# Expert phases of a two-block kernel: how 32 gathered rows are brought in, turned and multiplied

## The chip, the cores and the metric

The kernel runs on one core of one Trainium2 chip. The metric is the device time of one execution in microseconds; the median of three runs is 3614.87 us (3610.04 to 3619.33). Times inside the program come from one profiled execution, whose own time is 3593.02 us, with a span of 3591.0 us from its first instruction to its last.

## The reference, cut to what matters

The program is two transformer blocks in float32. The first block has two layers; each ends in a mixture of experts. Tokens (768 in layer 0, 512 in layer 1; model width 1024) each go to 2 of 32 experts; an expert has three matrices, two of 1024x512 and one of 512x1024:

```
def expert_block(a):
    xb, e = a
    return (jax.nn.silu(xb @ w1[e]) * (xb @ w3[e])) @ w2[e]

yb = lax.map(expert_block, (buf.reshape(n_blocks, MOE_BLOCK, d), blk_e)).reshape(n_blocks * MOE_BLOCK, d)
return jnp.zeros((t, d), h.dtype).at[tok_s].add(w_s[:, None].astype(h.dtype) * yb[dest])
```

How tokens are grouped into blocks is free as long as each token meets its own two experts.

## The kernel before

Program order: projections and attention of layer 0, routing, experts; the same for layer 1; then the second block. Only the two expert phases (function `expert_phase`), the load of the down weights (`load_down`, L1327) and one line at the end of routing (L1493) are touched.

Work of an expert phase is cut into units: one unit is 32 token slots of one expert. An expert has as many units as it needs, at least one. For each expert the weights w1, w3 and w2 (2 MB each) are read from HBM into one of four slots. SyncE issues the loads (L1321 for w1 and w3, L1327 for w2), in order: the loads of expert i wait until expert i-4 has finished with its slot (semaphores `hidden` and `multiplied`). The first three experts' loads are already issued in the routing phase. w1 and w3 are laid out so that a partition takes 8 neighbouring rows, 16 KB in one piece; w2 so that a partition takes 4 rows that lie 128 rows apart, 4 KB each.

One unit runs over the engines like this:

- GpSimd gathers 32 rows of `f` from HBM with one indirect DMA (L1565), 4 KB to each of 32 partitions; two buffers `xg` lie side by side on partitions 0 to 31 and 32 to 63. It is three units ahead of the one that TensorE works on.
- VectorE copies the rows to `x` (L1654), which frees the buffer. TensorE turns them, eight 32x128 transposes into PSUM (`turn_x`, L1600). ScalarE copies one half to `xT` (L1636), VectorE the other (L1658).
- TensorE multiplies with w1 and w3 into `pH` (L1615): 64 matmuls in the trace, four 32-column strips of the array at a time, so that hidden columns 0 to 127 stand on partitions 0 to 31, the next 128 on 32 to 63, and so on.
- ScalarE takes the silu (L1644), VectorE multiplies (L1668) into `hh`. TensorE turns `hh` as one 128x128 transpose (L1622), VectorE copies it to `hT` (L1671).
- TensorE multiplies with w2 into `pY` (L1627, 32 matmuls), ScalarE copies `pY` to `y` (L1648), and GpSimd scatters it to HBM (L1570): 128 pieces of 1 KB from 128 partitions.

TensorE turns the rows of the next unit between `pH` and `pT` of this one. The order on each engine is the order of the code; the loops run to counts read from `unit_end`, which routing has computed.

Of the kernel before, what the change touches and what calls it, by code (L numbers as in the profile page):

```python
# [18 lines left out]
ALU = mybir.AluOpType  # L19
# [1304 lines left out]
def load_down(sp, g, l, i, e):  # L1324

    b = i % SLOTS
    sp.dma_start(slot_of(g, "w2", b)[:], g["moe_w2"][l, e].rearrange("(k p) n -> p k n", p=P)).then_inc(g["w2_in"][b], 16)  # L1327


def routing_phase(nc, g, l, nt, logits, share, gather_at, scatter_at, unit_end):  # L1330
# [4 lines left out]
    with Phase(nc) as ph:  # L1335
# [68 lines left out]
        def _(dve):  # L1404
# [88 lines left out]
            dve.tensor_copy(gather_at[:, 0:NU], table[:, 0])  # L1493
# [7 lines left out]
def expert_phase(nc, g, l, nt, gather_at, scatter_at, unit_end):  # L1501


    T = nt * P
# [3 lines left out]
    half = C // 2  # L1508
    YW = D // STRIPS
    w13_in, w2_in = g["w13_in"], g["w2_in"]  # L1510
    with Phase(nc) as ph:
        at_x = ph.sb("at_x", [P, 2], I32)
        at_y = ph.sb("at_y", [P, 2], I32)
        xg = ph.sb("xg", [2 * UNIT, D])
        x = ph.sb("x", [UNIT, D])
# [3 lines left out]
        hT = ph.sb("hT", [P, P])  # L1519
        y = ph.sb("y", [P, 2, YW])  # L1520
        pX = [ph.ps(f"pX{h}", [P, 512]) for h in range(2)]
        pH = ph.ps("pH", [P, 512])
        pT = ph.ps("pT", [P, 512])
        pY = ph.ps("pY", [P, 512])
        x_ready, x_turned, x_movedA, x_movedD, hidden, silu, gated, h_turned, h_moved, multiplied, y_moved, order = (
            ph.sem(n) for n in ("x_ready", "x_turned", "x_movedA", "x_movedD", "hidden", "silu", "gated", "h_turned", "h_moved",
                                "multiplied", "y_moved", "order"))
        mark = ph.sem("mark")
# [3 lines left out]
        ident = g["ident"]  # L1532
# [25 lines left out]
        def _(pool):  # L1558
            last_row, last_out = pool.to_reg(T - 1), pool.to_reg(2 * STRIPS * T - 1)
            step = Steps(pool, order)  # L1560
            y_rows = g["y"][0:2 * T, :].rearrange("t (s n) -> (t s) n", s=STRIPS)

            def gather(u, b):
                step(pool.tensor_copy(at_x[:, b:b + 1], gather_at[:, ds(u, 1)]))  # L1564
                pool.indirect_dma_start(out=xg[strip(b)], out_offset=None, in_=g["f"][0:T, :],  # L1565
                                        in_offset=bass.IndirectOffsetOnAxis(ap=at_x[0:UNIT, b:b + 1], axis=0),
                                        bounds_check=last_row, oob_is_err=False).then_inc(x_in[b], 16)
# [11 lines left out]
            pool.wait_ge(x_ready, 1)  # L1579
# [16 lines left out]
        def _(pe):  # L1596
            def turn_x():
                for k in range(C):
                    j = k % half
                    last = pe.transpose(pX[k // half][:, j * UNIT:(j + 1) * UNIT], x[:, k::C], ident[0:UNIT, 0:UNIT])  # L1600
                last.then_inc(x_turned, 1)

            pe.wait_ge(x_ready, 1)
            turn_x()
            start = 0
            for i in range(NE):
# [3 lines left out]
                with pe.Fori(start, end) as u:  # L1610
                    pe.wait_ge(x_movedA, u + 1)
                    pe.wait_ge(x_movedD, u + 1)
# [5 lines left out]
                    pe.wait_ge(x_ready, u + 2)  # L1618
                    pe.sem_inc(mark, 1)
                    turn_x()  # L1620
# [12 lines left out]
        def _(act):  # L1633
            def move_x(n):
                act.wait_ge(x_turned, n)
                act.activation(xT[:, 0:half].rearrange("p k n -> p (k n)"), pX[0][:, 0:half * UNIT], ACT.Copy).then_inc(x_movedA, 1)  # L1636

            move_x(1)
            n = pairs_of(act)
            with act.Fori(0, n) as p:  # L1640
                for b in range(2):
# [3 lines left out]
                    move_x(u + 2)  # L1645
# [1276 lines left out]
```

## Time and profile before

| what | us |
|---|---|
| median of the runs | 3614.87 |
| profiled execution, its own time | 3593.02 |
| its span | 3591.0 |
| TensorE busy with matmuls, of the span | 3081.0 (86%) |
| expert phase of layer 0, about | 640 to 1201 |
| expert phase of layer 1, about | 1690 to 2222 |

A busy TensorE is one whose matmul records cover the time; it says nothing on how much of the array works. In the expert phases it covers less of the time than elsewhere, and the DMA engines, mostly idle in the rest of the program, are busy without a break. In the rows below, "idle before" is how long an engine did nothing before an instruction, and the name behind the arrow is what ended that. GB/s is all that the core's 16 DMA engines moved; their share can be a little over 1 since packets overlap. PEclk (the column "clock") is the granted clock of TensorE, 1.00 being 2.4 GHz.

### The profile page before, as it was taken

To read this page: it belongs to the slowest core of one execution; us is meant where nothing else is said; L and a number is where in the kernel's file an instruction comes from. 1 tells how busy PE (TensorE), PEld (TensorE's weight loads), DVE (VectorE), ACT (ScalarE), POOL (GpSimd) and SP (SyncE) were. 2 spreads that over 40 slices of the span, in tenths; PEclk is the share of its full clock that TensorE was granted. 3 is DMA by queue.
4 is the path that set the end of the run, shared out by engine and by line. 5 is a ranking of instruction groups with operands and counts; after the bars stand their busy time and mean duration, and the time that the engine had idled before them with its cause. 6 is when DMAs were issued, how large, how long until landed. Compare 5 with 4: busy or idle time off the path is not lost. (4 is left out here: it accounts for less than half of the span.)

```text
span 3591.0 us, 53246 instructions
## 1 busy us (share of the span) xinstructions
PE 3081.0 (86%) x22053; PEld 1770.0 (49%) x22053; DVE 1072.3 (30%) x2287; ACT 793.6 (22%) x1605; POOL 496.4 (14%) x608
## 2 busy tenths in 40 slices
PE   7998897878779699885978665599999999999999
PEld 4556654555446445653655443344444554444444
DVE  3425855211111333655111111543220321211101
ACT  2225630111112322630111111321111231110100
POOL 0004610222223100530222221000000000000000
PEclk8999997989889899996999887699999999999999
DMA  7823004999998541005999996321221111322337
GB/s 294 316 103 110 1 36 182 392 395 395 388 392 320 214 117 63 31 19 234 387 388 394 402 393 267 121 71 67 82 70 71 69 49 70 106 71 71 117 105 257
DMA packets 213104, 684.90 MB, mean 191 GB/s; under 512 B 51439, under 2 KB 92843, under 8 KB 196551
## 3 DMA queue, kind: packets, MB, share of 16 engines
q1 hardware_dynamic: 201126, 655.66, 49.0%
q0 software_dynamic: 11808, 26.78, 2.2%
q8 instruction: 132, 2.16, 0.2%
q14 instruction: 38, 0.30, 0.0%
HBM read 653.89 MB, written 33.98 MB: 192 GB/s over the span
## 5 line engine op out<-in xcount | busy, mean ns | idle before, releaser
L1615 PE MATMUL pH<-w,xT 128*32 128x256 f32 x7552 | 482.3, 411 | 161.0 <-DMA w<-in_moe_w 160.0
L1615 PEld LDWEIGHTS pH<-w,xT 128*32 128x32 f32 x7552 | 302.8, 119 | 322.2 <-issue 224.9
L2675 PE MATMUL banks<-hT,wf 128*128 128x512 f32 (+2 forms) x768 | 303.2, 557 | 3.3 <-ACT hT L2732 2.8
L1668 DVE TENSOR_TENSOR hh<-hs,pH 128x128 f32<-128x128 f32 x118 | 34.0, 288 | 833.9 <-ACT hs L1644 833.9
L1627 PE MATMUL pY<-w,hT 128*32 128x256 f32 x3776 | 230.3, 384 | 60.6 <-DVE hT L1671 51.3
L923 POOL TENSOR_SCALAR E<-E,st 128x768 f32<-128x768 f32 (+3 forms) x80 | 168.2, 2102 | 659.7 <-DVE st L1173 659.1
L2675 PEld LDWEIGHTS banks<-hT,wf 128*128 128x128 f32 x768 | 140.8, 190 | 164.6 <-issue 154.9
L416 PE MATMUL pa<-aT,w 128*128 128x512 f32 x416 | 207.6, 604 | 1.3 <-DVE aT L680 1.3
L1627 PEld LDWEIGHTS pY<-w,hT 128*32 128x32 f32 x3776 | 131.8, 110 | 124.3 <-issue 70.4
L2421 PE MATMUL pa<-hT,ring 128*128 128x512 f32 x384 | 167.8, 592 | 0.0
L2326 PE MATMUL pa<-hT,ring 128*128 128x512 f32 x384 | 165.0, 592 | 1.3 <-PEq L91 1.3
L968 PE MATMUL pT<-ident,E 128*128 128x128 f32 x672 | 113.0, 287 | 54.7 <-ACT PT L1078 31.1
L2714 PE MATMUL banks<-ring,aT 128*128 128x512 f32 x352 | 151.2, 592 | 0.0
L1600 PEld LDWEIGHTS pX<-ident,x 32*128 32x128 f32 x960 | 114.4, 197 | 72.1 <-issue 48.6
L1600 PE MATMUL pX<-ident,x 32*128 32x32 f32 x960 | 127.7, 273 | 22.7 <-DVE x L1654 22.7
L1970 PE MATMUL pa<-hT,ring 128*128 128x512 f32 x320 | 144.0, 606 | 2.7 <-issue 2.7
L1644 ACT ACTIVATE hs<-pH 128x128 f32<-128x128 f32 x118 | 32.8, 278 | 495.4 <-PE pH L1615 495.4
L998 PE MATMUL pS<-wout,oT 128*128 128x512 f32 x320 | 141.4, 594 | 0.8 <-issue 0.8
L1570 POOL DMA_INDIRECT y<-y,at_y x122 | 126.6, 1037 | 64.1 <-POOL at_y L1589 59.4
L1565 POOL DMA_INDIRECT xg<-f,at_x x124 | 117.4, 947 | 34.7 <-POOL at_x L1564 34.7
L968 PEld LDWEIGHTS pT<-ident,E 128*128 128x128 f32 x672 | 71.5, 142 | 100.0 <-issue 47.4
L2326 PEld LDWEIGHTS pa<-hT,ring 128*128 128x128 f32 x384 | 72.9, 190 | 93.4 <-issue 93.4
(445 smaller groups left out, 3954.8 us busy)
## 6 DMA issues: line engine op xcount, KB each, us to landing
w<-in_moe_w SPq DMA_DIRECT2D x192, 2048.0 KB, 35.4
mw<-in_mod_w SPq DMA_DIRECT2D x24, 2048.0 KB, 16.3
ring<-in_w_ff_down SPq DMA_DIRECT2D x33, 1024.0 KB, 4.9
ring<-in_w_in SPq DMA_DIRECT2D x15, 2048.0 KB, 8.4
ring<-in_w_gate SPq DMA_DIRECT2D x6, 2048.0 KB, 8.3
wf<-in_w_ff_gate SPq DMA_DIRECT2D x11, 1024.0 KB, 5.8
wf<-in_w_ff_up SPq DMA_DIRECT2D x11, 1024.0 KB, 8.2
w<-in_ab_w_in SPq DMA_DIRECT2D x6, 1024.0 KB, 6.4
```

The source lines that it names most:

```text
L416: last = pe.matmul(pa[n % 2][:, 0:512], w[:, i % SLOTS_W, k, tile(c)], aT[:, k, 0:512], start=(k == 0), stop=(k == C - 1))
L923: pool.tensor_scalar(e, e, st[:, u % 4, 6 + b:7 + b], None, ALU.mult).then_inc(readyP, 1)
L968: last = pe.transpose(pT[:, tile(j)], E[:, u % NB, b, tile(i)], ident[:])
L998: last = pe.matmul(pS[n % 2][:, half * 512:(half + 1) * 512], oT[:, k, tile(n)], wout[:, k, half * 512:(half + 1) * 512], start=(k == 4), ...
L1600: last = pe.transpose(pX[k // half][:, j * UNIT:(j + 1) * UNIT], x[:, k::C], ident[0:UNIT, 0:UNIT])
L1615: last = pe.matmul(pH[strip(s), 0:2 * P].rearrange("p (j n) -> p j n", j=2), xT[:, k, :], slot_of(g, "w13", b)[:, :, k, s * P:(s + 1) * P] ...
L1627: last = pe.matmul(pY[strip(s), 0:YW], hT[:, strip(k)], slot_of(g, "w2", b)[:, k, s * YW:(s + 1) * YW], start=(k == 0), stop=(k == HC - 1))
L1970: last = pe.matmul(pa[b][:], ring[:, j % RING, i, tile(c)], hT[:, i, :], start=(i == 0), stop=(i == C - 1))
L2326: last = pe.matmul(pa[b][:], ring[:, j % RING, i, at], hT[:, i, :], start=(i == 0), stop=(i == C - 1))
L2421: last = pe.matmul(pa[b][:], ring[:, j % RING, k, (c % 4) * P:(c % 4 + 1) * P], hT[:, k, :], start=(k == 0), stop=(k == C - 1))
L2675: last = pe.matmul(banks[f % 2][:, j * 512 + cols.start:j * 512 + cols.stop], wf[:, i % 2, j, k, (f % 2) * P:(f % 2 + 1) * P], hT[:, k, co ...
L2714: last = pe.matmul(banks[b][:, h * 512:(h + 1) * 512], aT[:, f, tile(t)], wd[:, m % SLOTS_D, f % 2, h * 512:(h + 1) * 512], start=(f == 0) ...
```

## The change

Four parts, all in the expert phases:

- The gather reads quarter rows: `f` is seen as rows of 256 numbers, and the indirect DMA brings 128 pieces of 1 KB to 128 partitions (quarter s of slot t to partition 32 s + t). Its indices are computed once in routing: 4 times the token number plus the partition's strip number (L1493).
- VectorE turns the gathered rows itself, in 32x32 blocks straight from `xg` to `xT`. The copy to `x`, TensorE's eight transposes, and both copies from PSUM go. The block turn of partition range s holds features 256 s to 256 s + 255, eight of them for each partition, which is the order in which w1 and w3 already lie.
- VectorE turns `hh` in 32x32 blocks too; TensorE's 128x128 transpose and the copy from PSUM go. This gives each partition four neighbouring hidden columns, so w2 is now laid out in that order.
- With that order w2 is 4 neighbouring rows per partition: 16 KB in one piece.

The semaphores x_ready, x_movedA, x_movedD, h_moved and mark go. The core of the diff:

```diff
-    sp.dma_start(slot_of(g, "w2", b)[:], g["moe_w2"][l, e].rearrange("(k p) n -> p k n", p=P)).then_inc(g["w2_in"][b], 16)
+    sp.dma_start(slot_of(g, "w2", b)[:], g["moe_w2"][l, e].rearrange("(p k) n -> p k n", p=P)).then_inc(g["w2_in"][b], 16)
...
-            dve.tensor_copy(gather_at[:, 0:NU], table[:, 0])
+            dve.tensor_scalar(gather_at[:, 0:NU], table[:, 0], float(STRIPS), strip[:], ALU.mult, ALU.add)
...
-        xg = ph.sb("xg", [2 * UNIT, D])
-        x = ph.sb("x", [UNIT, D])
+        xg = ph.sb("xg", [P, 2, XW])
...
-                pool.indirect_dma_start(out=xg[strip(b)], out_offset=None, in_=g["f"][0:T, :],
-                                        in_offset=bass.IndirectOffsetOnAxis(ap=at_x[0:UNIT, b:b + 1], axis=0),
+                pool.indirect_dma_start(out=xg[:, b], out_offset=None, in_=x_rows,
+                                        in_offset=bass.IndirectOffsetOnAxis(ap=at_x[:, b:b + 1], axis=0),
...
-                    pool.wait_ge(x_ready, 2 * p + b + 2)
+                    pool.wait_ge(x_turned, 2 * p + b + 2)
...
-                    pe.wait_ge(x_movedA, u + 1)
-                    pe.wait_ge(x_movedD, u + 1)
+                    pe.wait_ge(x_turned, u + 1)
...
-                    pe.wait_ge(x_ready, u + 2)
-                    pe.sem_inc(mark, 1)
-                    turn_x()
-                    pe.wait_ge(gated, u + 1)
-                    pe.transpose(pT[:, 0:P], hh[:], ident[:]).then_inc(h_turned, 1)
                     pe.wait_ge(w2_in[b], 16 * (loads_before(l, i) + 1))
-                    pe.wait_ge(h_moved, u + 1)
+                    pe.wait_ge(h_turned, u + 1)
...
-                            last = pe.matmul(pY[strip(s), 0:YW], hT[:, strip(k)], slot_of(g, "w2", b)[:, k, s * YW:(s + 1) * YW],
+                            last = pe.matmul(pY[strip(s), 0:YW], hT[:, k, :], slot_of(g, "w2", b)[:, k, s * YW:(s + 1) * YW],
...
-                    move_x(u + 2)
                     act.wait_ge(y_out[b], 16 * (p + 1))
...
-            def take_x(p, b):
+            def turn_x(p, b):
                 dve.wait_ge(x_in[b], 16 * (p + 1))
-                dve.tensor_copy(x[:], xg[strip(b)]).then_inc(x_ready, 1)
+                dve.transpose(xT[:], xg[:, b].rearrange("p (c k) -> p k c", k=C)).then_inc(x_turned, 1)
...
-                    take_x(p + b, 1 - b)
                     dve.wait_ge(silu, u + 1)
                     dve.tensor_tensor(hh[:], hs[:], pH[:, P:2 * P], ALU.mult).then_inc(gated, 1)
-                    move_x(u + 2)
-                    dve.wait_ge(h_turned, u + 1)
-                    dve.tensor_copy(hT[:], pT[:, 0:P]).then_inc(h_moved, 1)
+                    dve.wait_ge(gated, u + 1)
+                    dve.transpose(hT[:], hh[:].rearrange("p (c k) -> p k c", k=HC)).then_inc(h_turned, 1)
+                    turn_x(p + b, 1 - b)
```

What TensorE does for one unit of an expert (w_00 is the slot of its weights), in order, before:

```order
L1615 MATMUL pH<-w_00,xT 32x256 x32
L1618 REGISTER_ALU
L1600 MATMUL pX_4<-ident,x 128x32 x8
L1622 MATMUL pT<-ident,hh 128x128
L1627 MATMUL pY<-w_00,hT 32x256 x16
L1610 REGISTER_ALU
L1610 COMPARE_AND_BRANCH
```

and in the changed kernel:

```order
L1603 MATMUL pH<-w_00,xT 32x256 x32
L1610 MATMUL pY<-w_00,hT 32x256 x16
L1599 REGISTER_ALU
L1599 COMPARE_AND_BRANCH
```

Nothing stands between the two products any more; TensorE now waits there for VectorE.

What VectorE does for the first unit of a pair in the loop, before:

```order
L1654 COPY x<-xg 32x1024
L1667 ISA
L1668 TENSOR_TENSOR hh<-hs,pH 128x128
L1657 REGISTER_ALU
L1658 COPY xT<-pX_4 128x128
L1671 COPY hT<-pT 128x128
```

and in the changed kernel:

```order
L1639 TENSOR_TENSOR hh<-hs,pH 128x128
L1641 STREAM_TRANSPOSE hT<-hh 128x128
L1630 ISA
L1631 STREAM_TRANSPOSE xT<-xg 128x256
```

The rows of the next unit were taken ahead of `hh`; now they are turned behind `hT`, and the buffer `xg` is given back to GpSimd only then.

## Rows read from the trace of the kernel before

**Rows 1.** the page, costliest groups: shapes, count, busy us, mean ns, idle before.

```profile
L1615 PE MATMUL pH<-w,xT 128*32 128x256 f32 x7552 | 482.3, 411 | 161.0 <-DMA w<-in_moe_w 160.0
```

**Rows 2.** busy time by stretch: PE, PEld, DVE, ACT, POOL, clock, DMA share, GB/s.

```profile
1900.00:1950.00 50.00, 46.36 (x733) 31.97 (x729) 10.28 (x28) 11.71 (x25) 16.61 (x28) 1.00 1.02 383
1950.00:2000.00 50.00, 26.72 (x327) 15.47 (x319) 4.47 (x12) 5.77 (x12) 9.48 (x16) 0.81 1.01 404
1150.00:1175.00 25.00, 23.57 (x378) 16.61 (x370) 4.76 (x13) 5.66 (x12) 9.43 (x16) 1.00 0.18 59
```

**Rows 3.** timeline, one unit: start us, us, engine, line, names, count, idle before.

```profile
1167.04 1.06 PE L1600 MATMUL pX<-ident,x 32*128 32x32 f32 x8
1167.17 0.28 ACT L1644 ACTIVATE hs<-pH 128x128 f32<-128x128 f32 x1 [3.01 <-PE pH L1615]
1167.48 0.29 DVE L1668 TENSOR_TENSOR hh<-hs,pH 128x128 f32<-128x128 f32 x1 [5.31 <-ACT hs L1644]
...
1168.04 0.33 PE L1622 MATMUL pT<-ident,hh 128*128 128x128 f32 x1
...
1168.40 0.29 DVE L1671 COPY hT<-pT 128x128 f32<-128x128 f32 x1
1168.79 0.68 DVE L1654 COPY x<-xg 32x1024 f32<-32x1024 f32 x1
...
1168.84 1.93 PE L1627 MATMUL pY<-w,hT 128*32 128x256 f32 x32 [0.47 <-DVE hT L1671]
...
1170.62 3.66 PE L1615 MATMUL pH<-w,xT 128*32 128x256 f32 x64
```

**Rows 4.** by stretch, 0.7:3.7 and 4.2:7.0 us after a gather's issue (7 pairs).

```profile
1081.82:1084.82 3.00, 2.52 (x37) 1.97 (x40) 1.52 (x4) 0.51 (x2) 0.24 (x1) 1.00 0.96 406
1085.32:1088.12 2.80, 2.80 (x60) 2.04 (x53) 0.00 (x0) 1.67 (x2) 1.41 (x3) 1.00 1.01 335
...
1124.52:1127.52 3.00, 2.52 (x37) 1.97 (x40) 1.52 (x4) 0.50 (x2) 0.24 (x1) 1.00 0.97 401
1128.02:1130.82 2.80, 2.80 (x60) 2.04 (x53) 0.00 (x0) 1.67 (x2) 1.41 (x3) 1.00 0.97 315
```

**Rows 5.** DMA queues, 1097.65 to 1099.25: packets, MB, share of 16 engines.

```profile
DMA packets 89, 0.72 MB, mean 451 GB/s; under 512 B 6, under 2 KB 6, under 8 KB 58
...
q0 software_dynamic: 33, 0.12, 19.1%
```

**Rows 6.** DMA queues, 1099.55 to 1102.35.

```profile
DMA packets 114, 0.92 MB, mean 328 GB/s; under 512 B 25, under 2 KB 25, under 8 KB 69
...
q0 software_dynamic: 52, 0.13, 15.4%
```

**Rows 7.** groups by line, POOL: 640 to 1057, and 1690 to 2202.

```profile
L1565 POOL DMA_INDIRECT xg<-f,at_x x48 | 45.5, 948 | 13.6 <-POOL at_x L1564 13.6
...
L1565 POOL DMA_INDIRECT xg<-f,at_x x55 | 52.0, 946 | 15.4 <-POOL at_x L1564 15.4
```

**Rows 8.** timeline, TensorE: its last long wait in layer 0, and in layer 1.

```profile
1061.79 5.69 PE L1615 MATMUL pH<-w,xT 128*32 128x256 f32 x64 [7.33 <-DMA w<-in_moe_w]
...
2208.26 2.57 PE L1627 MATMUL pY<-w,hT 128*32 128x256 f32 x32 [1.89 <-DMA w<-in_moe_w]
```

**Rows 9.** groups by line, ACT, 1061.79 to 1201.

```profile
L1644 ACT ACTIVATE hs<-pH 128x128 f32<-128x128 f32 x19 | 5.3, 278 | 55.1 <-PE pH L1615 55.1
```

**Rows 10.** line L1321, first stretch: issue times, and issue to landing.

```profile
L1321 SPq DMA_DIRECT2D w<-in_moe_w x2: 532/722/913, 602.3 to 603.2; - x2
...
DMA to landing us min/median/max: 22.1/24.1/26.1
```

**Rows 11.** line L1321, the two loads after those.

```profile
L1321 SPq DMA_DIRECT2D w<-in_moe_w x2: 1197/5002/8806, 604.3 to 613.2; - x2
...
DMA to landing us min/median/max: 31.1/33.0/35.0
```

**Rows 12.** groups by line, DVE, 640 to 1201: a small SBUF operation.

```profile
L1498 DVE CAST scatter_at<-table 128x80 int32<-128x80 f32 x1 | 0.2, 203 | 0.0
```

More of the change, by code:

```diff
@@ L1507, in expert_phase @@
     ORDER = expert_order()
-    half = C // 2
-    YW = D // STRIPS
+    XW = YW = D // STRIPS
     w13_in, w2_in = g["w13_in"], g["w2_in"]
@@ L1518, in expert_phase @@
         hh = ph.sb("hh", [P, P])
-        hT = ph.sb("hT", [P, P])
+        hT = ph.sb("hT", [P, HC, UNIT])
         y = ph.sb("y", [P, 2, YW])
-        pX = [ph.ps(f"pX{h}", [P, 512]) for h in range(2)]
         pH = ph.ps("pH", [P, 512])
-        pT = ph.ps("pT", [P, 512])
         pY = ph.ps("pY", [P, 512])
[L1525 to L1528, printed above, removed]
+        x_turned, hidden, silu, gated, h_turned, multiplied, y_moved, order = (
+            ph.sem(n) for n in ("x_turned", "hidden", "silu", "gated", "h_turned", "multiplied", "y_moved", "order"))
         x_in, y_out = ([ph.stack.enter_context(nc.semaphore(f"unit_{n}{b}_{l}", num=Phase.FIRST - 8 + 4 * l + 2 * i + b)) for b in range(2)]
@@ L1531, in expert_phase @@
         block = ph.block()
-        ident = g["ident"]
         def end_of(eng, i):
@@ L1558, in _ @@
         def _(pool):
-            last_row, last_out = pool.to_reg(T - 1), pool.to_reg(2 * STRIPS * T - 1)
+            last_row, last_out = pool.to_reg(STRIPS * T - 1), pool.to_reg(2 * STRIPS * T - 1)
             step = Steps(pool, order)
+            x_rows = g["f"][0:T, :].rearrange("t (s n) -> (t s) n", s=STRIPS)
             y_rows = g["y"][0:2 * T, :].rearrange("t (s n) -> (t s) n", s=STRIPS)
@@ L1578, in _ @@
                 scatter(b)
-            pool.wait_ge(x_ready, 1)
+            pool.wait_ge(x_turned, 1)
             gather(2, 0)
@@ L1596, in _ @@
         def _(pe):
[L1597 to L1603, printed above, removed]
-            turn_x()
             start = 0
@@ L1617, in _ @@
                     last.then_inc(hidden, 1)
-                    pe.wait_ge(x_ready, u + 2)
-                    pe.sem_inc(mark, 1)
-                    turn_x()
-                    pe.wait_ge(gated, u + 1)
-                    pe.transpose(pT[:, 0:P], hh[:], ident[:]).then_inc(h_turned, 1)
                     pe.wait_ge(w2_in[b], 16 * (loads_before(l, i) + 1))
-                    pe.wait_ge(h_moved, u + 1)
+                    pe.wait_ge(h_turned, u + 1)
                     for k in range(HC):
                         for s in range(STRIPS):
-                            last = pe.matmul(pY[strip(s), 0:YW], hT[:, strip(k)], slot_of(g, "w2", b)[:, k, s * YW:(s + 1) * YW],
+                            last = pe.matmul(pY[strip(s), 0:YW], hT[:, k, :], slot_of(g, "w2", b)[:, k, s * YW:(s + 1) * YW],
                                              start=(k == 0), stop=(k == HC - 1))
@@ L1633, in _ @@
         def _(act):
[L1634 to L1638, printed above, removed]
             n = pairs_of(act)
@@ L1651, in _ @@
         def _(dve):
-            def take_x(p, b):
+            def turn_x(p, b):
                 dve.wait_ge(x_in[b], 16 * (p + 1))
-                dve.tensor_copy(x[:], xg[strip(b)]).then_inc(x_ready, 1)
-            def move_x(n):
-                dve.wait_ge(x_turned, n)
-                dve.tensor_copy(xT[:, half:C].rearrange("p k n -> p (k n)"), pX[1][:, 0:half * UNIT]).then_inc(x_movedD, 1)
-            take_x(0, 0)
-            move_x(1)
+                dve.transpose(xT[:], xg[:, b].rearrange("p (c k) -> p k c", k=C)).then_inc(x_turned, 1)
+            turn_x(0, 0)
             n = pairs_of(dve)
```

## The prediction, made before the changed kernel had run

> **What bounds the kernel now.** I began with the page's groups by cost. The largest is the first product of the experts, and it holds the one large wait of TensorE: 160.0 us for expert weights [rows 1]. The table of stretches says why: inside the expert phases the DMA engines are busy all the time, share 1.01 to 1.02, at 383 to 404 GB/s, whether TensorE is nearly full (46.36 of 50 us) or half idle (26.72) [rows 2]. So the weights set the pace, and the work of a unit lies beside them. Only the end of layer 0 is different: from 1150 on the DMA share is 0.18, while TensorE works on at 23.57 of 25 us [rows 2]. It waits for weights for the last time at 1061.79 [rows 8] and 19 units follow [rows 9]. In layer 1 it waits for a w2 as late as 2208.26 [rows 8]; there the end is one landing plus the unit and a half behind it. The phases thus have two prices: DMA time counts everywhere but in the last part of layer 0, and unit time counts almost only there.
>
> The third thing to see is that the rate is not constant. With 28 GpSimd entries (7 units) in 50 us it is 383 GB/s, with 16 (4 units) 404 [rows 2]. The bytes of the units are in both numbers, so three more units cost (404 - 383) x 50 / 3 = 350 KB each beyond what they move, 0.87 us at 404 GB/s. Cut finer: GpSimd issues a gather each 7.11 us where TensorE is the slower. From 0.7 to 3.7 us after an issue the seven rates, 406 in the first pair and 401 in the last, have a mean of 407; from 4.2 to 7.0 us after it, 335 to 315, mean 332 [rows 4]. The DMA view tells the two stretches apart. In the second half of the first one the software queue moves 0.12 MB and the total stays at 451 GB/s [rows 5]; in the second it moves 0.13 MB and the total is 328 [rows 6]. A unit has two software transfers of about 0.13 MB, scatter issued first, gather 1.5 us behind it, so the first is the scatter: 1 KB pieces from 128 partitions, free beyond its bytes. The second is the gather: 4 KB pieces to 32 partitions, and it costs (407 - 332) x 2.8 / 407 = 0.52 us of all DMA engines beyond its bytes.
>
> The Trainium skill has a rule for this (SBUF — State Buffer, section "Door 1: The DMA port swizzle"): what a DMA can move depends on how many of the 16 SBUF ports its partitions reach, and partitions 0 to 31 and 32 to 63 reach the same 8. By that rule a gather to 128 partitions reaches all 16 and the loss goes; the trace agrees so far as the scatter shows none.
>
> **Part 1, the gather over four partition ranges.** Its bytes stay; each transfer becomes like the scatter in pieces and partitions. If it behaves like it, 0.52 us a gather goes, in layer 0 for the 48 gathers issued before 1057, in layer 1 for the 55 before 2202 [rows 7]. Ends: 0.87 us gained [rows 2], or, as HBM is now read in 1 KB pieces, which no row shows, as much lost as is now lost, 0.52. I take 0.50: 24 us in layer 0, 27.5 in layer 1, as the scatter is the nearest row in every respect but direction. What is saved is seen in full, since loads queue behind one another without a gap.
>
> **Part 2, w2 in 16 KB pieces.** The first landings tell its worth. In a stretch free of units the second of two loads issued at 602.3 and 603.2 lands after 26.1, at 629.3 [rows 10]; the next w1 (issued 604.3, 35.0) at 639.3, its w3 (613.2, 31.1) at 644.3 [rows 11]. So a w2 and a w1 take 10.0 us together, and a w3 alone 5.0: 4 KB pieces cost nothing that I can read. I take 0, from -0.1 to +0.2 us for each of 58 loads, -6 to +12 us.
>
> The DMA page of the Trainium skill (DMA: Bandwidth & Descriptors, section "Why small descriptors are slow (HBM only)") speaks against part 1 and for part 2: some 3 cycles more for each piece, on 32 for 1 KB. By that estimate the gather would lose 0.02 us, 2 us in all; no run here shows a gather in 1 KB pieces.
>
> **Part 3, the turns.** Take the unit at 1167 [rows 3]. Silu ends at 1167.45, `hh` at 1167.77. Then TensorE's transpose (1168.04), VectorE's copy (to 1168.69), and the second product 0.15 later, at 1168.84. TensorE's eight transposes (1.06 us) lie beside silu and product and cost nothing; the 128x128 turn is what stands in the path. In the changed kernel VectorE turns `hh` at once: 0.03 us of waiting as between silu and `hh`, 0.29 as for the PSUM copy of the same shape, 0.15 to TensorE: second product at 1168.24, 0.60 earlier. No row shows a block turn; the ends are 0.20 (a small operation in SBUF [rows 12]) and 0.68 (the 32x1024 copy [rows 3]), so 0.69 to 0.21 gained. I take the copy of the same shape.
>
> The turn of the next rows, 256 numbers a partition, comes behind it and has to end before the next first product, 1.78 us after the second one begins [rows 3]; even 0.68 us fits. What waits behind it on VectorE is only the next `hh`, 4 us later. The loads of expert i+4 wait for `hidden`, which comes earlier.
>
> The gather is given its buffer one step later than before, after the turn in place of the copy; GpSimd issues it about 0.9 us after `hT`, and it is wanted two units later, some 12 us on. Its bytes fall within 4.2 to 7.0 us of issue [rows 4, 6], so it lies hidden, and if it ran late by more than 5 us it would hold `hh` too, as VectorE takes its work in order.
>
> Worth of part 3: 19 units behind the last wait of layer 0 [rows 9] x 0.60 = 11.4 us, and one turn behind the last landing of layer 1, 0.6 us. For the 99 others it only makes TensorE wait longer for weights. ScalarE's and VectorE's copies that go were never waited for; removing them is worth nothing. TensorE with longer pauses inside a unit could be granted less; in layer 0 after 1150 it is at 1.00 with 5.7% idle [rows 2], and the unit would be about 14% idle, so I keep 1.00 but not with certainty.
>
> **Sum.** 24 + 27.5 + 11.4 + 0.6 = 63.5 us, of the profiled execution's 3593.0: 3529.5. The runs shown have a median 21.8 above it, in parts of the program that are not touched so far as I can tell, so I take the same amount off that: 3614.87 - 63.5 = 3551. For the layer 0 terms to add, the weights of the last experts must not become the wait (the DMA share of 0.18 in the 25 us from 1150 [rows 2] puts the end of the loads near 1154 now, and 24 us sooner then; TensorE ends at 1201, and 35 us sooner then: 36 us remain between them, 47 now). They hold with room.
>
> **Rivals.**
>
> A. The loss in the second stretch is the reading's, not the partitions': rows scattered over HBM, and empty slots that all read row 0. For it: scatter and gather differ in direction too. Against: w2 is also read in 4 KB pieces, at full pace [rows 10, 11]. Then only 12 us go: 3603.
>
> B. The gather gets dearer. 128 pieces of 1 KB are read from HBM, and each gather costs 0.52 us more instead of less: 103 x 0.52 = 53.6 lost, 12 won, 41.6 slower: 3656. It is slower than before from 12 / 103 = 0.12 us a gather on. Against it: the scatter's 1 KB pieces are free [rows 5].
>
> C. Block turns are dear: VectorE reads with a stride, and `hh` takes four times the copy, 1.16 us. Then the second product comes 0.27 later than now, 5 us lost in 19 units where 11.4 were counted: 63.5 - 17 = 46 us: 3568.
>
> D. The clock. If the pauses bring TensorE down to its 1.2 GHz level in the last part of layer 0, a first product takes 5.7 us instead of 3.66, as the one at 1061.79 after a long wait [rows 8, 3]: 3 us a unit, some 50 us in 17 units, and the forecast shrinks to 3601.
>
> **How the numbers follow.** The forecast 0.58; a part of the DMA gain only (between it and A) 0.08; A 0.16; B 0.07; C 0.07; D 0.04. The forecast's own range is 3535 to 3570: 0.6 instead of 0.5 us a gather and the good end of w2 below, 0.4 us and the dear end of the turn above. The range for 8 in 10 is 3528 to 3604, which takes in A, C and D and leaves B out. 0.3%, about what can be told from no change, is 10.8 us, so the border is 3604; A lies on it and I split it, half faster, half the same. Faster: 0.58 + 0.08 + 0.08 + 0.07 + 0.02 = 0.83. Same: 0.08 and 0.02 of D, 0.10. Slower: 0.07.
>
> **What would show it.** Right: the stretch behind a gather as fast as the one before it, over 390 GB/s; layer 0's loads over 20 us sooner and layer 1's end over 25; a unit of 6.5 us after the last wait; block turns under 0.4 us, and none that a first product waits for. Packets under 8 KB fall by 32768, as w2 has no 4 KB packets more. Wrong: a dip of the same depth behind each gather (A), a deeper one (B), a second product over 1.7 us behind silu (C), clock under 1 at the end of layer 0 (D), or waits of `hh` for `xg`.

## The result, and the profile after

The changed kernel takes 3506.14 us (median of 4 runs, 3501.22 to 3511.0) where the kernel before takes 3614.41 (4 runs, 3610.04 to 3619.33): a ratio of 0.9689, 95% interval 0.9668 to 0.9710. It is 108 us faster. Forecast were 63.5, and the time lies below the range. The profiled executions, 3501.22 and 3593.02 (spans 3499.4 and 3591.0), are 91.8 apart. That pair is taken apart first; the other 16.5 us are treated further down, and it bears on them that 3593.02 is not one of the four runs of the kernel before and lies below all of them.

The page of the changed kernel: moved GB/s in the 40 slices, the packet count, the software queue, and the two products with the idle time ahead of them.

```profile
GB/s 299 314 118 113 1 21 135 423 423 423 423 424 295 217 121 85 11 19 246 422 422 423 424 424 273 42 73 63 89 72 72 49 49 72 109 72 88 105 110 262
DMA packets 188522, 684.82 MB, mean 196 GB/s; under 512 B 51438, under 2 KB 92842, under 8 KB 163782
...
q0 software_dynamic: 11808, 26.78, 2.0%
...
L1603 PE MATMUL pH<-w,xT 128*32 128x256 f32 x7552 | 478.5, 409 | 171.2 <-DMA w<-in_moe_w 148.2
...
L1610 PE MATMUL pY<-w,hT 128*32 128x256 f32 x3776 | 228.2, 381 | 150.2 <-DVE hT L1641 132.9
```

The first product still waits for weights, 148.2 us where it was 160.0 [rows 1], so the DMA engines still set the pace; but they move 422 to 424 GB/s in every full slice, whether many units run or few. Packets under 8 KB are 32769 fewer than before (196551), where 32768 were forecast for w2. The software queue, which carries gathers and scatters, has 11808 packets in both kernels, so that the trace does not show the size of the gathered pieces; that is known from the code only. The stretches show the steady rate against [rows 2] (columns as there), the last one mostly behind the last load:

```profile
700.00:750.00 50.00, 40.10 (x717) 26.93 (x713) 9.75 (x24) 10.04 (x19) 18.32 (x30) 1.00 1.01 422
750.00:800.00 50.00, 29.98 (x444) 17.28 (x440) 4.88 (x12) 5.60 (x11) 11.10 (x19) 0.80 1.01 423
900.00:950.00 50.00, 35.19 (x588) 21.27 (x592) 7.30 (x18) 7.82 (x15) 14.71 (x24) 0.94 1.01 424
1100.00:1150.00 50.00, 40.10 (x720) 27.02 (x716) 9.74 (x24) 10.04 (x19) 19.33 (x32) 1.00 0.32 125
```

The stretches 0.7 to 3.7 and 4.2 to 6.9 us after three gathers' issue (1049.80, 1056.42, 1063.05) answer to [rows 4]:

```profile
1050.50:1053.50 3.00, 3.00 (x62) 2.21 (x56) 0.00 (x0) 1.67 (x2) 1.51 (x3) 1.00 1.04 441
1054.00:1056.70 2.70, 1.50 (x28) 1.13 (x32) 1.22 (x3) 0.28 (x1) 0.46 (x2) 1.00 0.99 411
1057.12:1060.12 3.00, 3.00 (x63) 2.20 (x56) 0.00 (x0) 0.39 (x1) 1.56 (x3) 1.00 1.03 438
1060.62:1063.32 2.70, 1.49 (x28) 1.13 (x32) 1.22 (x3) 0.28 (x1) 0.46 (x2) 1.00 1.04 429
1063.75:1066.75 3.00, 3.00 (x62) 2.20 (x56) 0.00 (x0) 1.67 (x2) 1.52 (x3) 1.00 1.05 447
1067.25:1069.95 2.70, 1.50 (x28) 1.13 (x32) 1.22 (x3) 0.28 (x1) 0.46 (x2) 1.00 0.99 410
```

The dip behind a gather has shrunk from 407 against 332 to 442 against 417 in the mean, which is (442 - 417) x 2.7 / 442 = 0.15 us a gather instead of 0.52. It is a rough figure, of three gathers only.

One unit on the timeline, answering to [rows 3] (start, us, engine, line, names, idle before):

```profile
801.82 0.28 ACT L1622 ACTIVATE hs<-pH 128x128 f32<-128x128 f32 x1 [2.41 <-PE pH L1603]
802.12 0.29 DVE L1639 TENSOR_TENSOR hh<-hs,pH 128x128 f32<-128x128 f32 x1 [5.37 <-ACT hs L1622]
802.45 0.40 DVE L1641 STREAM_TRANSPOSE hT<-hh 128x128 f32<-128x128 f32 x1
802.77 0.61 DVE L1631 STREAM_TRANSPOSE xT<-xg 128x256 f32<-128x256 f32 x1
...
803.00 1.93 PE L1610 MATMUL pY<-w,hT 128*32 128x256 f32 x32 [1.24 <-DVE hT L1641]
...
804.22 1.04 POOL L1562 DMA_INDIRECT xg<-f,at_x  x1 [0.48 <-POOL at_x L1561]
...
804.72 3.66 PE L1603 MATMUL pH<-w,xT 128*32 128x256 f32 x64
```

From the start of the silu to the second product are 1.18 us (803.00 - 801.82) where there were 1.67 (1168.84 - 1167.17 in [rows 3]): 0.49 a unit. A unit takes 6.62 us, 7.11 before.

TensorE's last long waits, against [rows 8], layer 0 and then layer 1:

```profile
1027.55 6.52 PE L1603 MATMUL pH<-w,xT 128*32 128x256 f32 x64 [6.46 <-DMA w<-in_moe_w]
...
2129.30 1.93 PE L1610 MATMUL pY<-w,hT 128*32 128x256 f32 x32 [1.71 <-DMA w<-in_moe_w]
```

For all kernels I read these marks from the traces: the issue of the first expert load in layer 0 (s); the start of the first product behind the last long wait in layer 0 (a); the time from there to the end of the last `pY` of layer 0 (b); layer 1 from its first load's issue to its last `pY` (c), and, as a part of c, to the landing of its last w2, where TensorE waits for it or the trace has the landing (c'); and the time from the end of c to the end of the program (d). The last column is the profiled execution's own time.

| kernel | s | a | b | c | c' | d | time |
|---|---|---|---|---|---|---|---|
| before | 600.9 | 1061.8 | 137.5 | 557.4 | 546.6 | 1372.0 | 3593.0 |
| after | 599.1 | 1027.6 | 128.9 | 518.8 | 510.3 | 1361.5 | 3501.2 |
| e1 w2 alone | 598.3 | 1056.7 | 137.5 | 554.6 | 545.5 | 1374.8 | 3587.1 |
| e2 gather alone | 600.4 | 1036.8 | 137.8 | 527.3 | 518.3 | 1374.6 | 3541.2 |
| e3 gather and w2 | 601.2 | 1033.9 | 137.9 | 522.1 | 511.8 | 1372.7 | 3532.0 |
| e4 after, w2 in 4 KB | 598.4 | 1032.0 | 128.0 | 531.9 | 516.7 | 1361.5 | 3521.0 |
| e5 after, 32 neighbours | 598.8 | 1053.7 | 127.9 | 550.1 | 541.5 | 1365.1 | 3560.0 |
| e6 after, every fourth | 598.7 | 1024.7 | 128.6 | 516.0 | 507.4 | 1365.7 | 3498.5 |
| e7 before, one row | 597.9 | 1062.2 | 155.0 | 558.4 | - | 1373.1 | 3614.4 |
| e8 after, filler | 597.6 | 1031.6 | 134.8 | 524.1 | - | 1374.1 | 3532.4 |
| e9 after, no empty rows | 599.4 | 1027.2 | 127.6 | 515.7 | - | 1363.8 | 3501.6 |
| e10 after again | 597.2 | 1025.8 | 128.9 | 518.6 | 510.1 | 1365.3 | 3507.0 |
| e11 after again | 600.1 | 1028.7 | 128.9 | 518.8 | 510.3 | 1361.7 | 3502.5 |
| e12 as e6, again | 600.4 | 1027.7 | 128.1 | 516.2 | 507.6 | 1364.7 | 3500.1 |

Before to after: -34.2 in a, -8.6, -38.6 and -10.5, with +0.2 between the layers, -91.7. The forecast for these four was -24, -11.4, -28.1 and 0. In e1, e3, e4, e5, e6, e7 and e12 layer 1 is routed by other numbers than in the rest: it has as many units, spread over the experts in another way, so c and c' of these runs are less sure than a and b. The phase begins at another time in each run (s is 597 to 601), and a moves with it: e10 and e11 are the same kernel and have a 2.9 us apart, a - s only 0.1. So kernels are compared by a - s: 460.9 before and 428.5 after, 32.4 less.

### The profile page after: what moved, and what is told of

The parts are those of the page before. It is cut to its first block and busy times, and to the rows that moved or that the text cites. A ratio compares the mean times of both kernels' runs of the same rounds, so it can differ in the third digit from the quotient of the medians.

```text
span 3499.4 us, 50378 instructions
## 1 busy us (share of the span) xinstructions
PE 2918.9 (83%) x20975; PEld 1625.4 (46%) x20975; DVE 1041.1 (30%) x2167; ACT 760.2 (22%) x1485; POOL 508.0 (15%) x608
## 2 busy tenths in 40 slices
DMA packets 188522, 684.82 MB, mean 196 GB/s; under 512 B 51438, under 2 KB 92842, under 8 KB 163782
## 3 DMA queue, kind: packets, MB, share of 16 engines
q0 software_dynamic: 11808, 26.78, 2.0%
## 5 line engine op out<-in xcount | busy, mean ns | idle before, releaser
L1603 PE MATMUL pH<-w,xT 128*32 128x256 f32 x7552 | 478.5, 409 | 171.2 <-DMA w<-in_moe_w 148.2
L1603 PEld LDWEIGHTS pH<-w,xT 128*32 128x32 f32 x7552 | 292.5, 118 | 338.7 <-issue 211.8
L1562 POOL DMA_INDIRECT xg<-f,at_x x124 | 129.6, 1045 | 62.0 <-POOL at_x L1561 58.9
L1625 ACT ACTIVATE y<-pY 128x256 f32<-128x256 f32 x118 | 45.4, 384 | 418.6 <-PE pY L1610 418.6
L1561 POOL COPY at_x<-gather_at 128x1 int32 (+1 forms) x124 | 23.0, 186 | 747.0 <-DVE xT L1631 472.1
L937 PE MATMUL pS<-kT,qT 64*128 64x256 f32 (+2 forms) x608 | 110.1, 479 | 8.4 <-ACT E L1067 4.9
```

The source lines that it names most:

```text
L1562: pool.indirect_dma_start(out=xg[:, b], out_offset=None, in_=x_rows, in_offset=bass.IndirectOffsetOnAxis(ap=at_x[:, b:b + 1], axis=0), bou ...
L1603: last = pe.matmul(pH[strip(s), 0:2 * P].rearrange("p (j n) -> p j n", j=2), xT[:, k, :], slot_of(g, "w13", b)[:, :, k, s * P:(s + 1) * P] ...
```

## The experiments

**The parts alone.** The kernel before with one or two of the parts. In e1 and e3 (and e4) w2's rows meet hidden columns in another order than their own, so that outputs differ from the reference's and layer 1 is routed by other numbers; it still has 54 units, as all others.

e1, in the kernel before:

```diff
-    sp.dma_start(slot_of(g, "w2", b)[:], g["moe_w2"][l, e].rearrange("(k p) n -> p k n", p=P))...
+    sp.dma_start(slot_of(g, "w2", b)[:], g["moe_w2"][l, e].rearrange("(p k) n -> p k n", p=P))...
```

> The kernel before with w2 loaded in 16 KB pieces alone. Its rows then meet the wrong hidden columns (that is left as it is), so layer 0 can be compared, while layer 1 is routed otherwise and its number of units may differ. Theory G: layer 0 ends at 1199 as before, give or take 3 us, and the stretches of layer 0 stay at 383 to 404 GB/s. Theory W: about 10 us earlier, 1189.

e2, in the kernel before (gather and indices as in the change, one copy to `x` for each partition range):

```diff
-                dve.tensor_copy(x[:], xg[strip(b)]).then_inc(x_ready, 1)
+                for s in range(STRIPS):
+                    last = dve.tensor_copy(x[:, s * YW:(s + 1) * YW], xg[strip(s), b])
+                last.then_inc(x_ready, 1)
```

> The kernel before with one part of the change: the gather in 1 KB pieces to 128 partitions. VectorE then puts the four quarters side by side into x (four copies of 32x256 in place of one of 32x1024), TensorE turns as before, w2 in 4 KB pieces. The change as a whole moved the last w13 wait of layer 0 34 us up and shortened layer 1 by 38 us. Theory G (all of the DMA gain is the gather's, 0.7 us each): layer 0 ends at about 1165 instead of 1199, the DMA engines move 415 to 424 GB/s in full stretches, whole run 72 us under before, about 3542. Theory W (0.5 us a gather and 0.3 to 0.4 us for each w2 in 16 KB pieces): layer 0 ends at 1175, whole run 51 us under before, 3563. Theory T (the rate rose because TensorE's turns and their copies are gone, not by the DMA's shape): no change, 3614.

e3 is e2 with e1's line.

> The kernel before with both: gather to 128 partitions and w2 in 16 KB pieces, turns still by TensorE; w2 again meets wrong columns, so only layer 0 is compared. Theory G: layer 0 ends as in the run with the gather alone, about 1165. Theory W: 10 us earlier than with the gather alone (1165 against 1175). Theory T: 1199.

e4 is the changed kernel with w2 in the old order, 4 KB pieces.

> The changed kernel with w2 loaded in 4 KB pieces as before (it meets wrong hidden columns; only layer 0 is compared). Theory G: layer 0 ends at 1157 as in the changed kernel. Theory W: 10 us later, 1167, with lower GB/s wherever a w2 is under way.

All four ran on one chip, with the kernel before at 3590.67 us (7 runs, 3587.21 to 3593.21). e2: 3537.76 (4 runs, 3536.79 to 3541.16), ratio 0.9853, interval 0.9836 to 0.9869, 53 us faster. One run each: e1 3587.07, e3 3532.03, e4 3521.04. The gather alone brings a - s from 460.9 to 436.4 and c' from 546.6 to 518.3, 24.5 and 28.3 us: 0.51 us a gather in both layers, for 48 and 55.

The expectations fared as follows. For e2, theory W's 51 us under before and layer 0's end at 1175 fit (53 us, a + b = 1174.5), G's 72 us do not, and T is out. For e1, layer 0 ends at 1194.2, 5 us before G's 1199 and 5 behind W's 1189, 2.6 of the 5 by its earlier start. For e3, it ends at 1171.8 and not at W's 1165, since TensorE holds up the loads there (below). For e4, it ends at 1160.0, between G's 1157 and W's 1167, with the lower rate that W expected. So W had the gather right, and the worth of w2 in layer 0 lies between the two.

Stretches of e2, then of e3, then of e4; the first of e2 and of e3 is the point:

```profile
700.00:750.00 50.00, 46.67 (x738) 33.17 (x739) 13.41 (x49) 10.61 (x25) 17.51 (x29) 1.00 0.97 394
900.00:950.00 50.00, 42.08 (x629) 28.46 (x621) 10.67 (x39) 9.21 (x20) 14.80 (x24) 0.93 1.01 418
```

```profile
700.00:750.00 50.00, 46.67 (x746) 33.13 (x739) 13.39 (x49) 10.41 (x24) 17.46 (x29) 1.00 0.93 383
900.00:950.00 50.00, 42.12 (x634) 29.20 (x638) 11.85 (x45) 9.48 (x21) 14.76 (x24) 0.97 1.01 423
```

```profile
610.00:640.00 30.00, 19.08 (x71) 14.25 (x71) 15.82 (x80) 0.00 (x0) 0.19 (x1) 0.67 1.01 420
...
700.00:750.00 50.00, 41.30 (x740) 28.15 (x744) 8.91 (x22) 10.13 (x19) 18.82 (x32) 1.00 1.02 419
900.00:950.00 50.00, 35.29 (x576) 22.12 (x576) 7.28 (x18) 7.81 (x15) 14.65 (x24) 0.90 1.01 419
```

Two things follow. With w2 in 4 KB the full rate is 418 to 419, with 16 KB it is 423. And with TensorE's old unit (e2, e3) the DMA share falls to 0.97 and 0.93 between 700 and 750, where the changed kernel has 1.01: TensorE, at 46.67 of 50 us and with a unit of 7.11 us, does not free the slots fast enough for the faster loads. In e3 this costs (422 - 383) x 50 / 422 = 4.6 us; from e3 to the changed kernel a - s falls by 4.2. In e2 it costs (417 - 394) x 50 / 417 = 2.8 us, 417 being the rate of the stretches around it; from e2 to e4, which is the same step with w2 in 4 KB, a - s falls by 2.8.

**What in the gather was dear.** e5 and e6 are the changed kernel with gathers of 32 whole rows, 4 KB each, once to 32 neighbouring partitions and once to every fourth of all 128. The turn reads the first 256 numbers of every partition of the buffer, so that part of the rows does not enter; the indices are those of the kernel before, GpSimd zeroes the buffer once, and work and bytes are the same.

```diff
-                pool.indirect_dma_start(out=xg[:, b], out_offset=None, in_=x_rows,
+                pool.indirect_dma_start(out=xg[strip(b), b], ..., in_=g["f"][0:T, :],      # e5
+                pool.indirect_dma_start(out=xg[0:P:STRIPS, b], ..., in_=g["f"][0:T, :],    # e6, e12
```

> The changed kernel with the gather as before: 32 rows of 4 KB, into partitions 0 to 31 or 32 to 63. VectorE turns a 128x256 view of the buffer all the same, so its numbers are not the rows' (only layer 0 is compared). If the gather's shape sets the loss: layer 0 ends about 25 us later than in the changed kernel (1181 against 1156.5) and stretches fall to 385 to 400 GB/s. If the turns were it: 1157.

> As the last one, but the 32 rows of 4 KB go to every fourth partition of 128. Theory P (the loss comes of the 32 neighbouring partitions that the pieces land in): as in the changed kernel, 1157, 420 GB/s. Theory R (it comes of reading 4 KB rows, or of the size of the pieces): as with 32 neighbouring partitions, 1181.

> The changed kernel with the gather as 32 pieces of 4 KB to every fourth partition, timed over several rounds. The turn then reads the first 256 numbers of the buffer's partitions, so that three quarters of the rows do not enter and the output is not the reference's; the work is the same in kind and amount. Theory S (what costs is that the 32 destination partitions are neighbours): 3490 to 3507, the changed kernel or a little under it, since 32 larger pieces are fewer packets than 128. Rival W (the number of partitions written is what counts, 128 against 32): some 50 us over the changed kernel.

e5 took 3560.0, e6 3498.46 (one run each, on the chip of e10). e12, on the chip of e11, has a median of 3499.90 (5 runs, 3494.21 to 3500.17) beside e11's 3505.90 (5 runs, 3502.49 to 3508.81). Stretches of e5, then of e6:

```profile
700.00:750.00 50.00, 40.10 (x720) 26.86 (x714) 9.39 (x24) 10.05 (x19) 17.59 (x30) 1.00 1.01 387
```

```profile
700.00:750.00 50.00, 40.10 (x720) 26.96 (x716) 9.75 (x24) 10.04 (x19) 17.80 (x30) 1.00 1.01 421
950.00:1000.00 50.00, 36.00 (x588) 22.36 (x581) 7.31 (x18) 7.82 (x15) 13.17 (x23) 0.89 1.01 427
```

Pieces, bytes, source and count are the same in both, only the destination differs, and with it 387 against 421 GB/s. By a - s (454.9 against 426.1) and c' (541.5 against 507.4) the neighbours cost 28.8 and 34.1 us, 0.60 and 0.62 us a gather. Neither size nor number of pieces explains it: 32 pieces of 4 KB do a little better than 128 of 1 KB once they are spread, 425 to 427 against 422 to 425 in the stretches from 750 to 1050, and the median of e12 is 6.0 us under that of e11. The rule of the Trainium skill named in the prediction (SBUF — State Buffer, section "Door 1: The DMA port swizzle") agrees with this pair.

**What is read.** e7 is the kernel before with all gather indices 0, so that every slot of every unit reads the same row:

```diff
-            dve.tensor_copy(gather_at[:, 0:NU], table[:, 0])
+            dve.tensor_scalar(gather_at[:, 0:NU], table[:, 0], 0.0, None, ALU.mult)
```

> The kernel before with every gather index 0: all 32 slots of a unit read the same row of HBM (the products are then of that row, and layer 1 routes otherwise; only layer 0 is compared). Theory P: no change, layer 0 ends at 1199, 383 to 404 GB/s. Theory R, in the form that the empty slots, which all read row 0, make the gather slow: slower still, 1215 or more.

It took 3614.43, the kernel before on the same chip 3614.63 (7 runs, 3613.11 to 3619.43). Its loads come no sooner than in the trace of before: c is 558.4 and 557.4, a - s even 3.4 us more, most likely lost between 700 and 750, where the granted clock is 0.92 and the DMA share falls to 0.92. In the stretches with a full share it moves 390 to 398 GB/s between 750 and 1050, where before has 383 to 399. So scattered rows are not the loss. Its late end of layer 0 (b 155.0, so 1217, as theory R had it) I first took for a price of reading one row; the rows of the clock, below, say otherwise.

e9 is the changed kernel with the indices of empty slots out of bounds, so that nothing is fetched for them (GpSimd zeroes the buffer once):

```diff
+            step(dve.scalar_tensor_tensor(out=table[:, 0], in0=table[:, 0], scalar=float(STRIPS), in1=table[:, 1], op0=ALU.mult, op1=ALU.add))
+            step(dve.tensor_scalar(gather_at[:, 0:NU], table[:, 0], strip[:], None, ALU.add))
```

> The changed kernel with the gather indices of empty slots out of bounds, so that no row is fetched for them; the row buffer is zeroed once by GpSimd. Theory G (a gather now costs hardly more than its bytes): a slot left out saves only its 4 KB; with about half of the slots empty that is some 0.1 us of all DMA engines a unit, 5 us of layer 0 and 6 of layer 1: 5 to 11 us under the changed kernel of this call. Rival R (empty slots that all read row 0 still cost something of their own, as the run with one row for every slot hints): 15 us or more under it. If it is the same within 3 us, the descriptors that are skipped cost as much as those that are moved.

> The changed kernel once more, as the measure for the others of this call. If the kernel before is at 3614 here, 3507; if it is at 3591, then 3483 if the chips differ by a constant, and about 3500 if the change also removes what makes the kernel before differ from chip to chip.

e9's median is 3503.52 (5 runs, 3499.78 to 3506.04), 2.4 under e11's, with the ranges of the two overlapping. 684.82 - 679.07 = 5.75 MB less are moved, 13.6 us at 423 GB/s, and layer 0 and 1 are only 2.8 and 3.1 us shorter. The median alone would fit the expectation's last case, that a skipped row costs as much as a fetched one. The software queue says that it does not; between 640 and 1115 and between 1680 and 2130, in e9 and then in e11:

```profile
q0 software_dynamic: 5712, 11.47, 6.4%
q0 software_dynamic: 4883, 7.75, 4.7%
```

```profile
q0 software_dynamic: 5707, 13.43, 7.3%
q0 software_dynamic: 4890, 10.59, 6.1%
```

That is 0.9% of 475 us and 1.4% of 450 us, about 10.6 us of all DMA engines for 4.80 MB, and 4.80 MB are 11.3 us at 423 GB/s: the time goes with the bytes, as in theory G. It is mostly not seen because something else is late: in layer 1 the last wait for weights is then at 2106.42, with four second products of TensorE behind it, where e11 waits for the last w2 until 2130.40; and in layer 0 the DMA share between 1050 and 1100 is 0.94 instead of 0.97.

**The kernels once more, on two chips.**

> The changed kernel again, so that it stands on the chip of these runs beside the kernel before. The first chip gave 3506 against 3614, a second one had the kernel before at 3591. If the change takes off what the phases of the profile lost (42.8 us in layer 0, 38.5 in layer 1, some 10 behind them), 92 us: 3499 where before is 3591. If the whole 108 us belong to the change: 3483.

e10 has 3507.32 (4 runs, 3506.75 to 3507.7) beside 3614.63 of the kernel before, ratio 0.9700, interval 0.9684 to 0.9717. e11, on a third chip, has 3505.90 beside 3590.20 (9 runs, 3582.08 to 3597.66), ratio 0.9768, interval 0.9754 to 0.9782. The changed kernel is the same on both within 1.5 us; the kernel before differs by 24. Of the cases in the expectations the first of e11's holds on e10's chip (3507), and on e11's the last one (about 3500) is the nearest, 6 us off; a constant difference of the chips (3483) is out.

**The part behind the experts.** In the changed kernel with this diff nothing waits for the increments:

```diff
                 pe.wait_ge(w13_in[b], 32 * (loads_before(l, i) + 1))
+                for _ in range(10):
+                    pe.sem_inc(mark, 1)
```

> The changed kernel with ten semaphore increments more on TensorE at the start of each expert, 320 a layer, that nobody waits for. They move all TensorE code behind them to another place in the instruction stream and change nothing else. Theory P (the stretch from the last second product of layer 1 to the end is shorter in the changed kernel because TensorE's code there lies at other places, and one stop for instructions with a clock drop behind it is gone): that stretch is 1371 to 1375 us again, as in all kernels with TensorE's old expert code, or at any rate not 1361 to 1366. Rival (the shorter stretch has another cause, such as what the experts leave behind in time or memory): 1361 to 1366 as in every kernel with the new code. Should the stretch stay, position is not thereby excluded, since stops need not come at each new place. Expert phases: layer 0 at most 2 us later (increments are issued while TensorE waits for weights, except for the last four experts).

Column d is 1374.1, where it is 1361.5 to 1365.7 in the eight other runs with the new TensorE code and 1372.0 to 1374.8 in the five with the old. Stops of TensorE that wait for nothing but instructions, in e8 and then in the trace of before:

```profile
2304.83 0.37 PE L1983 MATMUL pD<-A 64*32 64x32 f32 x6 [4.68 <-issue]
2412.67 0.36 PE L1979 MATMUL pD<-q,k 64*32 64x32 f32 x15 [4.20 <-issue]
```

```profile
2472.99 0.63 PE L2009 MATMUL pD<-A 64*32 64x32 f32 x15 [4.45 <-issue]
```

The changed kernel has no stop of over 1.7 us there. Behind the stop the granted clock of the kernel before falls, and the next 32 products take 16.41 us, where they take 14.00 in the changed kernel:

```profile
2472.00:2482.00 10.00, 9.01 (x36) 4.48 (x36) 2.48 (x3) 0.92 (x3) 1.16 (x4) 0.66 0.23 90
...
2474.18 16.41 PE L1970 MATMUL pa<-hT,ring 128*128 128x512 f32 x32
```

```profile
2386.56 14.00 PE L1941 MATMUL pa<-hT,ring 128*128 128x512 f32 x32
```

So where TensorE's code lies is enough to make d as long as with the old code, and nothing that it computes there differs. That the place is also what shortens d in the changed kernel follows from this and from the stops, which all five traces with the old code have (4.15 to 4.45 us) and none of the eight others; which place stops and which does not, I can't say. I expected at most 2 us from the increments in the expert phases; they cost 5.4 in a - s, 5.9 in b and 5.4 in c, against e10 and e11. The rows say why: ahead of an expert's first product TensorE stands 1.1 us in issue, five such rows in b.

```profile
1102.43 3.66 PE L1606 MATMUL pH<-w,xT 128*32 128x256 f32 x64 [1.14 <-issue]
```

## Why the prediction was wrong

**The direction, the cause and the gather's size were right.** The gather was forecast at 24 and 27.5 us and brings 24.5 and 28.3 by itself (e2). The view that named it, [rows 4 to 6], was read rightly: what cost was that its partitions are neighbours (e5 against e6). Rival A is out by e5 against e6 and by e7; B by e2.

**The main step that failed** is "for the 99 others it only makes TensorE wait longer for weights", together with w2 at 0: what I called hidden stood beside loads of the old speed. From the kernel before over e2 and e3 to the changed kernel, a - s falls by 24.5 (gather), 3.7 (w2) and 4.2 (turns), and c' by 28.3, 6.5 and 1.5; over e4 instead of e3 the turns are worth 2.8 and 1.6, w2 5.1 and 6.4. So the turns bring 4 to 6 us where the prediction had nothing, and w2 10 to 12. For the two phases I had asked what waits last in the kernel before, and not once more in the kernel with the faster gather. The trace of before holds the hint: from its first product, at 651.67, TensorE works 16 units in a row before it waits for weights for the first time:

```profile
768.65 3.66 PE L1615 MATMUL pH<-w,xT 128*32 128x256 f32 x64 [0.57 <-DMA w<-in_moe_w]
```

An expert of three units keeps TensorE for 3 x 7.11 = 21.3 us, and its 6.29 MB with 0.26 for each unit pass in 18.5 us at 383 GB/s and in 17.4 at the 407 of [rows 4] (16.8 at the 422 found since), so a few such experts in a row use up the lead that four slots give, and sooner at the higher rate. The share of 0.93 in e3 is that, and its 4.6 us are about what the turns then bring, 4.2.

In layer 1 the rest of c, behind the last landing, is 10.7 us before and 8.6 after, 2.2 less where 0.6 was forecast. One turn of `hh` is 0.5 of it, as e2 to the changed kernel shows (9.1 to 8.6); the other 1.7 are clock, for the second product [rows 8] and the first one behind it take 2.57 and 4.76 us in the trace of before, 1.93 and 3.64 in the changed kernel.

**w2 in 16 KB pieces** was forecast at 0, with ends of -6 and +12. With the new gather it is worth 10.2 us by e3 against e2 and 10.6 by the changed kernel against e4 (5.1 in a - s, 6.4 in c', -0.9 in b); in the kernel before, by e1, only 3.6. The whole of c must not be used for it: e4's is 13.1 us above the changed kernel's, but its layer 1, routed by other numbers, has one unit more behind the last landing:

```profile
2142.47 1.93 PE L1610 MATMUL pY<-w,hT 128*32 128x256 f32 x32 [1.67 <-DMA w<-in_moe_w]
```

From there to the end of its last `pY` are 15.2 us, where the changed kernel has 8.6 (2129.30 to 2137.87). The two landings of [rows 10, 11] could not show it: several loads are under way at once (issued from 600.9 to 604.3, the last of them landing at 644.3), and 0.25 us are lost in the difference of two landings. The stretch free of units does show it, in the changed kernel and in the kernel before, as in e4 above:

```profile
610.00:640.00 30.00, 19.82 (x74) 14.90 (x74) 15.82 (x81) 0.00 (x0) 0.00 (x0) 0.66 1.01 429
```

```profile
610.00:640.00 30.00, 20.86 (x78) 16.00 (x78) 16.17 (x83) 0.21 (x1) 0.00 (x0) 0.63 1.01 424
```

With 4 KB pieces it is 424, 422 (e2) and 420 (e4), with 16 KB 429, 428 (e1) and 430 (e3). Over 14.9 us of an expert's loads 7 in 422 are 0.25 us a w2, 14 for the 58; the 10.2 and 10.6 above are 0.18. SyncE shows the same: the third issue of w1 and w3 takes 10.04 us in the kernel before and 0.94 in the changed one, 9.96 and 10.04 in e2 and e4 with 4 KB pieces, 0.99 and 0.96 in e1 and e3 with 16 KB. Why, no run shows; the loads behind it came on time.

```profile
604.32 10.04 SPq L1321 DMA_DIRECT2D w<-in_moe_w  x2
```

```profile
602.10 0.94 SPq L1321 DMA_DIRECT2D w<-in_moe_w  x2
```

**The turn of `hh`** was forecast at 0.29 us and takes 0.40; a unit gains 0.49 instead of 0.60, 9.3 us in 19 units, and b falls by 8.6 instead of 11.4; 0.8 of it are lost again as b's first product, behind the long wait, takes 6.52 us and not 5.69. The step was right, its size a little off. For the turn of x, under 0.68 was forecast; it takes 0.60. Groups of the changed kernel, VectorE, 640 to 1157:

```profile
L1631 DVE STREAM_TRANSPOSE xT<-xg 128x256 f32<-128x256 f32 x65 | 39.3, 604 | 8.9 <-DMA xg<-f,at_x 8.9
L1641 DVE STREAM_TRANSPOSE hT<-hh 128x128 f32<-128x128 f32 x64 | 25.8, 403 | 2.2
L1639 DVE TENSOR_TENSOR hh<-hs,pH 128x128 f32<-128x128 f32 x64 | 18.4, 287 | 425.9 <-ACT hs L1622 425.9
```

`hh` waits for nothing but the silu, so the order of work on VectorE did no harm; the turn of x waits once, 8.9 us, for the first gather. Rival C (1.16 us) had the right sign, with 0.11 us more than forecast instead of 0.87.

**The rest of the program** was forecast as untouched: it is 10.5 us shorter, by e8 from the place of the code. No row of before would have told on which side it falls; the stop of 4.45 us could have told that there was something to lose or gain.

**"The same amount off that"**: I took the 21.8 us between the runs' median and the profiled execution as a constant. It is 21.4 before and 4.9 after, which is the other 16.5 us. The 3593.02 lies among the runs on the chips where the kernel before takes 3590 (3582.08 to 3597.66) and outside those of the 3614 (3610.04 to 3619.43), and its mean granted clock, 0.937, lies among theirs as well (below). So it was most likely taken on a chip of another kind than the runs; the record does not name its chip. e7, the old TensorE code on the chip where the kernel before takes 3614.63, shows where such time goes. The window from the end of the first product behind the last long wait in layer 0 to the layer's end, of e7 and then of before:

```profile
1068.09:1217.20 149.11, 133.88 (x1932) 92.76 (x1931) 26.68 (x75) 28.07 (x65) 42.81 (x72) 0.93 0.60 230
```

```profile
1067.48:1199.30 131.82, 122.79 (x1931) 87.10 (x1931) 27.38 (x75) 29.02 (x65) 42.73 (x72) 1.00 0.68 257
```

The same instructions, 17.3 us more, and the granted clock is 0.93 instead of 1.00. In e7's timeline the clock falls to its 1.2 GHz level for a few us at a time, in the middle of units, at 1158, 1182 and 1199 among others, and with no gap ahead of it that other units do not have as well. TensorE had been busy for 89% of the time from 1068 to 1182 (93% in the row of before, 122.79 of 131.82). One of the falls, a second product of 3.12 us instead of 1.93 and a first of 4.25 instead of 3.66:

```profile
1182.20 3.12 PE L1627 MATMUL pY<-w,hT 128*32 128x256 f32 x32 [0.48 <-DVE hT L1671]
1185.02 4.25 PE L1615 MATMUL pH<-w,xT 128*32 128x256 f32 x64
```

e10, the changed kernel on that chip:

```profile
1033.00:1154.70 121.70, 98.90 (x1760) 66.69 (x1760) 22.75 (x56) 23.43 (x45) 44.91 (x74) 1.00 0.66 270
```

81% busy, and the clock stays at 1.00. So rival D had it the wrong way round: longer pauses in a unit cost no clock, and on this chip the kernel with them keeps it where the one without them does not. That the pauses are the reason fits these rows and is not shown, as no run changes them alone; nor is there a trace of the kernel before itself on this chip. The mean granted clock of the runs bears it out for the kernel before: 0.925 to 0.929 in the seven runs of 3614.63 (e7 has 0.929), 0.935 to 0.939 in those of 3590.67 and 3590.20, and 0.935 to 0.938 for the changed kernel on the first of these chips. For the runs at the top it is an inference, from their times alone, that their chip was of the first kind.

The error of 45 us is then 8.4 in a - s and 1.8 by the earlier start, which is chance, -2.8 in b, 10.5 in c, 10.5 in d, and 16.5 in the step from the profiled execution to the median. The two terms that the sum had, gather and turn of `hh`, each came out within 3 us of their forecast. The range was too narrow below chiefly as all my doubts pointed upward.

## What to carry to other kernels

When the resource that sets the pace gets faster, ask again, with the new rates, what is late next; an edit that looks worth nothing alone (the turns) or little (larger pieces, 3.6 us) then adds. The reverse holds as well: where something else is late, saved DMA time is not seen (e9). Let an indirect gather beside a full stream of loads write to partitions spread over all 128; here that held for pieces of 1 KB and of 4 KB. Compare traces from the start of the phase, and leave out what lies behind it and depends on the data. A difference between a median and a profiled execution can itself be a cost with a place, and need not survive the change.

## What was unexpected of the hardware

- Destination alone: 32 pieces of 4 KB to neighbouring partitions take 0.6 us of all DMA engines more than to every fourth partition (387 against 421 GB/s, e5 and e6).
- A gathered row that is skipped by an index out of bounds takes hardly any time: the software queue's time falls with its bytes, 10.6 us for 4.80 MB (e9).
- VectorE turns 128x128 f32 in 32x32 blocks in 403 ns, against 0.29 us for a PSUM copy of that shape. The Trainium skill (VectorE: DVE Perf Modes, section "The three transpose paths") has 311 ns for bf16; no run here shows bf16.
- Ten semaphore increments cost TensorE 1.1 us ahead of an expert (e8), and moving its code made stops of 4.2 and 4.7 us elsewhere: 8 to 13 us of a part whose work is the same.
- The same TensorE code had a granted clock of 1.00 or 0.93 in the same stretch on different chips (before and e7), without a gap ahead of the falls; the changed kernel kept 1.00 in that stretch on the chip where e7 lost it (e10).
